# All mixture-of-experts blocks placed by matmul, 34 blocks a pass in place of 40, some split 96 and 32 rows

## The chip, the core and the metric

One core of one Trainium2 chip runs the whole step. The metric is device time in microseconds from one launch. Five engines work side by side: PE (TensorE; its weight loads are shown apart as PEld), DVE (VectorE), ACT (ScalarE), POOL (GpSimd) and SP (SyncE, which only issues DMAs here). Sixteen DMA engines serve the core.

## What is computed

The reference is one layer of a hybrid diffusion backbone over 128 context and 256 latent tokens of width 1024: attention and a recurrent branch, then a mixture of experts, then a final norm. The change is in the mixture of experts:

```python
t = h.reshape(B * T, D)                       # 384 tokens in all, D = 1024
# sigmoid routing, group-limited, TOP_K = 8 of N_EXPERTS = 64 -> gates (n, 64)
act = silu(einsum('nd,edf->nef', t, w_gate_e)) * einsum('nd,edf->nef', t, w_up_e) * gates[:, :, None]
routed = einsum('nef,efd->nd', act, w_down_e) # expert width 256
shared = (silu(t @ w_gate_s) * (t @ w_up_s)) @ w_down_s
x = x + gate_ffn * (routed + shared)
```

So 384 x 8 = 3072 token rows go to 64 experts of unequal load, and every expert's 3 MB of fp32 weights (w_gate, w_up, w_down, 1 MB each) come from HBM once.

## The kernel before

Stages. Up to about 335 us the kernel computes the adaLN vectors, the projections, attention, the recurrent branch and the merge. Around 340 us it routes: a count of each expert's rows, a sort of the experts by load, and tables from which every block of rows is picked. From 360 us on it works through blocks of 128 rows, in turns. The last 20 us are the final norm and the store.

Blocks. The experts are taken in four groups of 16. A block is of kind H (128 rows of one heavy expert) or L (64 rows each of two experts). A group is 4 H and 6 L, so 10 turns (`ORDER0` for the first group, `ORDER` for the others), and a pass is 40 turns. If an expert had more rows than its place holds, a further pass would run (`limits`, `more_i`); the runs here need one.

One turn, u, on PE, in program order: `gate_up(u)` (L1538: x_t against w_gate and w_up, 8 steps of the contraction, 512 columns moving; for H one matmul of 128 stationary columns a step, for L two of 64, on the two halves of the array, which write partitions 0-63 and 64-127 of one bank); `turn_tokens(u+1)` (L1526, 8 transposes of the next block's gathered rows); `down(u-1)` (L1557: 2 halves of 512 columns by 2 contraction steps, split by rows as above); two transposes of the activation (L1666); `block_rows(u+3)` (L1519, a small product that finds row numbers and gates of a later block); and, for a placed block, `place(u-1)` (L1576). An fp32 matmul stands in the trace as two records; an fp32r one, as in `place`, as one.

How a block's result returns to its tokens. There are two ways. A scattered block is scaled by its gates (ACT, y_sb) and added into y_dram by an indirect DMA that POOL issues (L792); each scatter waits until the one before has landed. y_dram is zeroed first (L713, 3 MB) and at the end read back in six DMAs of 512 KB (L599, L600) and summed by DVE. A placed block is split into a high and a low fp32r part (ACT L1094, DVE L2236) and multiplied by a 0/1 matrix made by DVE (L2224, token number against row): 3 token tiles x 2 halves x high and low = 12 matmuls of 128x512 (L1576); DVE then adds six banks into ffn_acc (L2247). 17 of the 40 blocks are placed: two of the first group (`FIRST_PLACED`), five of each later group (`PLACED`; in the last group `ENDING`, two of whose five are done in `place_ending`, L1601). 23 are scattered.

Order and buffers. Weights arrive in a ring of five slots of 3 MB (`ring`, `gu`, `dn`). SP issues an expert's w_gate and w_up when the slot's last user has finished `gate_up`, w_down when it has finished `down`. `gate_up(u+1)` writes a bank that the placement of the turn before used, so it waits for DVE's first sum; `turn_tokens` waits for all six. The shared expert's down product (`shared_down`, L1452) runs in turns 5, 6 and 7 of the first group, and the broadcast of gate_ffn (`spread`, L1189) in turn 4.

A place where the array is cut into 32-column tiles is L1178, in the adaLN stage: four matmuls of 32 stationary columns, 512 moving, on four quarters of the array.

Of the kernel before, what the change touches and what calls it, by code (L numbers as in the profile page):

```python
# [5 lines left out]
F32 = mybir.dt.float32  # L6
# [28 lines left out]
ORDER0, ORDER = "HHHHLLLLLL", "HLLHLHLLHL"  # L35
NGRP, EPG, BPG = 4, 16, 10
NPASS_BLK = NGRP * BPG
MAXPASS = 4
# [3 lines left out]
NBLK = NPASS_BLK * MAXPASS  # L42
NSIDE = 2 * NPASS_BLK
FIXED = 4
PLACED = (0, 2, 4, 5, 7)
SCATTERED = BPG - len(PLACED)
FIRST_PLACED = (BPG - 3, BPG - 2)
ENDING = (0, 2, BPG - 3, BPG - 2, BPG - 1)
HEAVY = 16
EMPTY = 1024  # L50
MARK = 4096.0
TABLES = 3 + 7
RC = 387
LAT0 = 131
NTAB = NBLK + 4
# [11 lines left out]
def hybrid_step(nc, x_prompt, x_sample, cache_k, cache_v, state_f, state_b, c, c_ctx,  # L67
# [5 lines left out]
    with ctx:  # L73
        KB = 1024
        arena = ctx.enter_context(nc.sbuf_tensor("arena", [P, 207 * 256 + 160], F32))
# [124 lines left out]
        shared_dn = at("shared_dn", [P, 2048], EX + 48)  # L200
# [4 lines left out]
        shared_sb = at("shared_sb", [P, D], EX + 56)  # L205
        x_t = at("x_t", [P, KD * CAP], EX + 108)
        zeros = at("zeros", [P, D], EX + 108)
        a_sh = at("a_sh", [P, TT, 2 * CAP], EX + 112)
        y_sb = [at(f"y_sb{i}", [P, D], EX + 116 + 4 * i) for i in range(2)]
# [31 lines left out]
        shift = little("shift", [P, 2, NSIDE])  # L241
        row_off = little("row_off", [P, 1])
        slot_row = little("slot_row", [P, UN], I32)
# [13 lines left out]
        seq_rank = little("seq_rank", [NE, NE])  # L257
        side_pick = little("side_pick", [NE, NSIDE])
        seq_pick = little("seq_pick", [NE, NE])
        inv_cap = little("inv_cap", [P, NSIDE])  # L260
        fill = little("fill", [P, NSIDE])
        place[0] = EX + 162.5
        limit[0] = EX + 163.5
        seq_expert = little("seq_expert", [1, MAXPASS * NE], I32)


        ffn = [at(f"ffn{t}", [P, D], EX + 4 * t) for t in range(TT)]
        ffn_b = [at(f"ffn_b{t}", [P, D], EX + 12 + 4 * t) for t in range(TT)]
# [3 lines left out]
        y_r = [at(f"y_r{i}", [P, D], EX + 116 + 4 * i, F32R) for i in range(2)]  # L272
        y_hi = [y_r[0], at("y_hi", [P, D], EX + 36, F32R)]
        y_lo_end = at("y_lo_end", [P, D], 12, F32R)
        y_lo = [at(f"y_lo{i}", [P, D], EX + 44 - 4 * i, F32R) for i in range(2)]
# [5 lines left out]

        y_dram = nc.dram_tensor("y_dram", (2 * NTOK, D), F32, kind="Internal").ap()

# [30 lines left out]
        for n, (kind, i) in enumerate(chunks):  # L314
# [3 lines left out]
        S = {n: sem(n) for n in """added cond_loaded vec_loaded cache_loaded bias_loaded block_loaded  # L318
# [10 lines left out]
            gates_made sides_mm sides_evac picks_made sorted_mm gu_used dn_used b_zero  # L329
            sh_mm sh_silu sh_act sh_at_mm sh_at shd_mm shd_evac shared_loaded early_mm  # L330
# [25 lines left out]
        def experts_of(order):  # L356

            n, blocks = 0, []
            for kind in order:
                blocks.append(tuple(range(n, n + 1 + (kind == "L"))))  # L360
                n += len(blocks[-1])
            assert n == EPG
            return blocks
# [3 lines left out]
        def shared_turn(u, first):  # L367

            return (u - FIRST_SHARED,) if first and FIRST_SHARED <= u < FIRST_SHARED + TT else ()

        def shared_outs(u):

            return bank[2 + (u + 1) % 2], bank[2 + u % 2]

        FIRST_SHARED = 5
        SHARED_BANK = (2, 3, 5)
        SPREAD_TURN = 4
# [5 lines left out]

        first_half = (("router_loaded", 16), ("shared_loaded", 48), ("bias_loaded", 32))

        def heavy_places(order):
            return [x[0] for x, kind in zip(experts_of(order), order) if kind == "H"]

        FIRST_FOUR = heavy_places(ORDER0)


        SLOT0 = [x % RING for x in range(EPG)]
        heavy_slot, light_slots = 3, (1, 2, 4, 0)
        SLOT, lights = [], 0
        for x in range(EPG):
            if x in heavy_places(ORDER):
                SLOT.append(heavy_slot)
            else:
                SLOT.append(light_slots[lights % 4])
                lights += 1  # L400
# [20 lines left out]
        assert not {SLOT[x] for x in turns[False][-1]} & {1, 2}  # L421
        assert [SLOT0[x] for x in turns[False][-1]] == [SLOT[x] for x in turns[False][-1]]

        assert max(PLACED) < UN - 2

        assert {SLOT[x] for x in turns[False][UN - 3]} == {1, 2}
        assert not {SLOT[x] for u in (UN - 2, UN - 1) for x in turns[False][u]} & {1, 2}

        def placed_in(last):
            return ENDING if last else PLACED  # L430

        def is_placed(u, first, last=False):
            return u in FIRST_PLACED if first else u % UN in placed_in(last and u >= 0)

        def first_scatters(u):

            return 16 * sum(v not in FIRST_PLACED for v in range(u))

        def scatters_ahead(b, u, last=False):

            back = 1 if u < 0 else 0
            here = placed_in(last and not back)
            return b * (16 * SCATTERED) + 16 * (len(PLACED) - len(FIRST_PLACED) - SCATTERED * back + sum(v not in here for v in range(u % UN)))

        def places_ahead(b, v, each, last=False, first=False):

            if first:
                return each * FIRST_PLACED.index(v)
            return b * (each * len(PLACED)) + each * (placed_in(last).index(v) + len(FIRST_PLACED) - len(PLACED))

        def low_rows(v, last):

            return y_lo_end if last and v == UN - 3 else y_r[1 - v % 2]
# [4 lines left out]

        def rows_of(x, order_x):

            return slice(0, P) if len(order_x) == 1 else slice(HALF * order_x.index(x), HALF * order_x.index(x) + HALF)
# [34 lines left out]
        def _(sp):  # L496
# [37 lines left out]
            def load_gu(x, group, e):  # L534
                k, y = slot_of(x, group is None), earlier(x, group is None)
                if group is None:
                    if y is not None:
                        sp.wait_ge(S["gu_used"], y + 1)
                    elif k == RING - 1:
                        sp.wait_ge(S["sh_mm"], TT)  # L540
                else:
                    sp.wait_ge(S["gu_used"], group * EPG + (y + 1))
                    sp.sem_inc(S["sp_turn"], 1)
# [4 lines left out]
            def load_dn(x, group, e):  # L548
                k, y = slot_of(x, group is None), earlier(x, group is None)
                if group is None:  # L550
                    if y is not None:
                        sp.wait_ge(S["dn_used"], y + 1)
                else:
                    sp.wait_ge(S["dn_used"], group * EPG + (y + 1))
                    sp.sem_inc(S["sp_turn"], 1)
# [6 lines left out]
            for g, w in enumerate((w_gate_s, w_up_s)):  # L562
                sp.dma_start(shared_gu[:, 2048 * g:2048 * g + 2048], w[0].rearrange("(p k) n -> p (k n)", k=KD)).then_inc(S["shared_loaded"], 16)
            sp.wait_ge(S["out_mm"], 12)
            for n, x in enumerate(FIRST_FOUR):
                if n == FIXED - 1:

                    sp.wait_ge(S["sides_mm"], 1)
                    sp.wait_ge(S["h2_stored"], 16 * TT)
# [5 lines left out]
            for u in range(BPG):  # L575
                now = [(x, expert_at(slice(x, x + 1))) for x in turns[True][u] if x not in FIRST_FOUR]
                for n, (x, e) in enumerate(now):
                    load_gu(x, None, e)
                    if x == FIXED:
                        sp.dma_start(shared_dn[:, :], w_down_s[0].rearrange("(p k) n -> p (k n)", k=2)).then_inc(S["shared_loaded"], 16)  # L580
# [4 lines left out]
            with sp.Fori(1, passes * NGRP) as b:  # L585
                late = [(x, expert_at(bass.ds(b * EPG + (x - EPG), 1))) for x in turns[False][-1]]
                for u in range(BPG):
                    now = [(x, expert_at(bass.ds(b * EPG + x, 1))) for x in turns[False][u]]
# [5 lines left out]
            sp.wait_ge(S["added"], scatters_ahead(passes * NGRP - 1, UN - 1, True))  # L594
            sp.sem_inc(S["sp_turn"], 1)
            sp.wait_ge(S["dn_used"], (passes * NGRP - 1) * EPG + (turns[False][UN - 3][-1] + 1))
            sp.sem_inc(S["sp_turn"], 1)
            for t in range(TT):
                sp.dma_start(ffn[t][:, :], y_dram[t * P:(t + 1) * P, :]).then_inc(S[first_half[t][0]], 16)  # L599
                sp.dma_start(ffn_b[t][:, :], y_dram[NTOK + t * P:NTOK + (t + 1) * P, :]).then_inc(rows_loaded[t], 16)  # L600
            for x in turns[False][-1]:
                load_dn(x, passes * NGRP - 1, expert_at(bass.ds(passes * NE + (x - EPG), 1)))
# [6 lines left out]
        def _(pool):  # L609
# [101 lines left out]
            pool.memset(zeros[:, :], 0.0).then_inc(S["zero_filled"], 1)  # L711
            pool.wait_ge(S["zero_filled"], 7)
            pool.dma_start(y_dram.rearrange("(t p) d -> p t d", p=P), zeros[:, :].unsqueeze(1).to_broadcast([P, 2 * TT, D])  # L713
                           ).then_inc(S["b_zero"], 16)
# [23 lines left out]
            late = NE - EPG  # L738
            side = lambda ap: ap[:, 2 * BPG:NSIDE].rearrange("p (g u h) -> p g u h", u=BPG // 2, h=2)
# [1545 lines left out]
```

## Time and profile before

| | |
|---|---|
| median of 3 runs | 927.61 us |
| lowest, highest | 926.42, 934.16 us |
| span of the profiled execution, first to last instruction | 925.6 us |
| median over the span | 2.0 us |
| PE busy | 876.7 us, 95% of the span |
| DMA moved | 294.24 MB, mean 318 GB/s |

In the rows, busy time is the union of an engine's instructions; matmuls overlap and their ends are modelled, so the distance between starts is the surer measure. In a line of the time order, `128*64 128x512 ... x32` is 32 records with 128 rows and 64 columns of the array in use and 512 moving columns, and the number in brackets is idle time before the line and what ended it.

### The profile page before, as it was taken

What the parts mean: (1) busy time and instruction counts of PE and PEld (TensorE: products, weight loads), DVE (VectorE), ACT (ScalarE), POOL (GpSimd) and SP (SyncE); (2) the same over time, 40 slices, a digit from 0 to 9 for tenths busy, and PEclk for the clock granted to TensorE, in tenths of its full rate; (3) what the DMA queues carried; (4) which work ended last, traced back from release to release, by engine and by line L of the source; (5) the groups of instructions that cost most, each with busy time, mean ns of one, the idle gap of its engine ahead of it and who ended that gap; (6) DMA issues with size and microseconds to landing.
All of it is one profiled execution on the core that took longest, in us unless ns stands there. A gap on an engine that the chain in (4) does not pass through costs nothing.

```text
span 925.6 us, 12174 instructions
## 1 busy us (share of the span) xinstructions
PE 876.7 (95%) x4185; PEld 513.0 (55%) x4185; DVE 436.2 (47%) x961; ACT 254.9 (28%) x417; POOL 138.6 (15%) x224
## 2 busy tenths in 40 slices
PE   4799999999999899999999999999999999999991
PEld 2387876899998765443344444444444444444440
DVE  1562493677666554233253442542344442433386
ACT  2536634444423431212211122122112112212211
POOL 7410000000002131122110111011111012012202
PEclk9799999999999999999999999999999999999996
DMA  9974885722237398899999999999999999999971
GB/s 353 350 266 172 302 292 211 159 92 65 79 131 267 138 417 310 271 348 406 379 404 420 404 401 402 421 391 406 409 408 409 421 394 408 411 407 400 404 319 68
DMA packets 82416, 294.24 MB, mean 318 GB/s; under 512 B 16876, under 2 KB 33320, under 8 KB 57408
## 3 DMA queue, kind: packets, MB, share of 16 engines
q1 hardware_dynamic: 62352, 263.21, 71.7%
q0 software_dynamic: 11312, 25.85, 9.4%
q10 hardware_dynamic: 8704, 4.54, 1.9%
q8 instruction: 30, 0.49, 0.2%
q14 instruction: 18, 0.15, 0.0%
HBM read 286.11 MB, written 20.71 MB: 332 GB/s over the span
## 4 chain that ended last, share of the span: by engine, by line
PE 75%; DMA 14%; DVE 4%; issue 3%; ACT 1%; SPq 0%; ACTq 0%; POOL 0%; DVEq 0%; POOLq 0%
PE bank L1538 26%; PE bank L1557 13%; PE bank L1150 8%; PE bank L1152 7%; PE bank L1151 7%; DMA y_dram<-y_sb,slot_row 5%; PE bank L1526 4%; DMA chunk_raw<-in_w_ada_dram 3%; DMA b_t<-in_b_ada_dram 2%; PE bank L1178 1%; DMA h_dram<-h_row 1%; DMA dn<-in_w_down_e_dram 1%; PE bank L1230 1%; PE bank L1452 1%; DMA xg<-h_dram,slot_tok 1%
## 5 line engine op out<-in xcount | busy, mean ns | idle before, releaser
L1538 PE MATMUL bank<-gu,x_t 128*64 128x512 f32 (+1 forms) x1024 | 283.8, 596 | 2.6 <-DVE ffn_acc L2247 1.8
L1538 PEld LDWEIGHTS bank<-gu,x_t 128*64 128x64 f32 (+1 forms) x1024 | 101.3, 150 | 160.7 <-issue 157.4
L1557 PE MATMUL bank<-dn,a_t 128*64 128x512 f32 (+1 forms) x512 | 145.4, 597 | 0.6 <-DMA dn<-in_w_down_e_dram 0.6
L2113 DVE TENSOR_TENSOR act_sb<-silu_sb,bank 128x256 f32<-128x256 f32 x40 | 16.8, 421 | 194.8 <-ACT silu_sb L1111 194.8
L1111 ACT ACTIVATE silu_sb<-bank 128x256 f32<-128x256 f32 x40 | 15.4, 385 | 316.1 <-PE bank L1538 316.1
L1557 PEld LDWEIGHTS bank<-dn,a_t 128*64 128x64 f32 (+1 forms) x512 | 48.5, 150 | 69.8 <-issue 68.8
L1150 PE MATMUL bank<-h_hi,chunk_lo 128*128 128x384 f32 x240 | 84.2, 351 | 0.0
L1152 PE MATMUL bank<-h_hi,chunk_hi 128*128 128x384 f32 x240 | 80.6, 336 | 0.0
L1151 PE MATMUL bank<-h_lo,chunk_hi 128*128 128x384 f32 x240 | 80.4, 335 | 0.0
L792 POOL DMA_INDIRECT y_dram<-y_sb,slot_row x23 | 38.5, 1674 | 259.7 <-DVE slot_row L1996 225.7
L780 POOL DMA_INDIRECT xg<-h_dram,slot_tok x40 | 41.5, 1037 | 197.5 <-DVE slot_row L1996 175.5
L475 DVE TENSOR_TENSOR chunk_lo<-chunk_raw,chunk_hi 128x2048 fp32r<-128x2048 f32 x25 | 57.1, 2287 | 15.8 <-ACT chunk_hi L469 15.7
L469 ACT ACTIVATE chunk_hi<-chunk_raw 128x2048 fp32r<-128x2048 f32 x25 | 47.7, 1914 | 42.5 <-PE bank L1152 42.3
L2129 DVE COPY a_t<-bank 128x256 f32<-128x256 f32 x40 | 16.9, 423 | 76.8 <-PE bank L1666 76.6
L1526 PEld LDWEIGHTS bank<-ident,xg 128*128 128x128 f32 x320 | 35.5, 140 | 27.3 <-issue 26.6
L1150 PEld LDWEIGHTS bank<-h_hi,chunk_lo 128*128 128x128 f32 x240 | 45.0, 188 | 7.1 <-issue 5.4
L2247 DVE TENSOR_TENSOR ffn_acc<-ffn_acc,bank 128x512 f32<-128x512 f32 x78 | 47.8, 683 | 0.4
L1576 PE MATMUL bank<-y_r,place_r 128*128 128x512 f32 x174 | 45.1, 401 | 1.2 <-DVE a_t L2129 1.1
L1094 ACT ACTIVATE y_sb<-bank,slot_gate 128x512 f32<-128x512 f32 x46 | 31.6, 687 | 51.9 <-PE bank L1557 50.6
L1151 PEld LDWEIGHTS bank<-h_lo,chunk_hi 128*128 128x128 f32 x240 | 45.1, 188 | 0.3
L1152 PEld LDWEIGHTS bank<-h_hi,chunk_hi 128*128 128x128 f32 x240 | 45.1, 188 | 0.0
L1526 PE MATMUL bank<-ident,xg 128*128 128x128 f32 x320 | 42.8, 277 | 0.6 <-DMA xg<-h_dram,slot_tok 0.6
(366 smaller groups left out, 1099.9 us busy)
## 6 DMA issues: line engine op xcount, KB each, us to landing
gu<-in_w_gate_e_dram SPq DMA_DIRECT2D x64, 1024.0 KB, 14.7
gu<-in_w_up_e_dram SPq DMA_DIRECT2D x64, 1024.0 KB, 18.1
dn<-in_w_down_e_dram SPq DMA_DIRECT2D x64, 1024.0 KB, 19.5
chunk_raw<-in_w_ada_dram SPq DMA_DIRECT2D x24, 1024.0 KB, 8.8
chunk_raw<-in_w_in_dram SPq DMA_DIRECT2D x18, 1024.0 KB, 5.4
chunk_raw<-in_w_out_dram SPq DMA_DIRECT2D x4, 1024.0 KB, 5.1
y_dram<-zeros POOLq DMA_DIRECT2D x1, 3072.0 KB, 18.6
chunk_raw<-in_w_pa_dram SPq DMA_DIRECT2D x2, 1024.0 KB, 5.1
```

The lines of the kernel that those rows point to most:

```text
L469: act.activation(chunk_hi[j % HIGHS][:, :], chunk_raw[slot[n]][:, :], ACT.Copy).then_inc(S["chunk_high"], 1)
L475: dve.tensor_tensor(chunk_lo[slot[n]][:, :], chunk_raw[slot[n]][:, :], chunk_hi[j % HIGHS][:, :].bitcast(F32), ALU.subtract).then_inc(S["c ...
L780: pool.indirect_dma_start(xg[u % 2][:, :], None, h2_dram[:, :], bass.IndirectOffsetOnAxis(ap=slot_tok[:, u % UN:u % UN + 1], axis=0), boun ...
L792: pool.indirect_dma_start(y_dram[:, :], bass.IndirectOffsetOnAxis(ap=slot_row[:, u % UN:u % UN + 1], axis=0), y_sb[u % 2][:, :], None, bou ...
L1150: pe.matmul(out, left[1], right[0], start=start, stop=False)
L1151: pe.matmul(out, left[0], right[1], start=False, stop=False)
L1152: return pe.matmul(out, left[0], right[0], start=False, stop=stop)
L1526: mm = pe.transpose(bank[k // 4][:, (k % 4) * P:(k % 4 + 1) * P], xg[u % 2][:, k * P:(k + 1) * P], ident[:, :])
L1538: mm = pe.matmul(bank[2 + u % 2][at_x, :].rearrange("p (g n) -> p g n", g=2), x_t[:, cols], wide[:, :, k, :], start=(k == 0), stop=(k == K ...
L1557: mm = pe.matmul(outs[half][at_x, :], a_t[:, cols], dn[slot_of(x, first)][:, wc], start=(k == 0), stop=(k == 1))
L1576: return pe.matmul(out[:, :], place_r[:, t * P:(t + 1) * P], y[:, halves[half]], start=start, stop=not start)
L2247: dve.tensor_tensor(ffn_acc[t][:, cols], ffn_acc[t][:, cols], out[:, :], ALU.add).then_inc(S["place_out"], 1)
```

## The change

All 34 blocks of a pass are placed; the scatters, y_sb, y_dram, its zeroing, its reading back and the sums over it are gone. There is a new kind, M: 96 rows of one expert and 32 rows of another. The first group is MMMHHLHLHL (10 turns), the others are MLLMLLML (8 turns each): 4 H, 12 M and 18 L. The 96 rows of an M run as a tile of 64 columns and one of 32, the 32 rows as a tile of 32 columns, so each step of `gate_up` and `down` is three matmuls, in the order 64, 32, 32.

The heavy experts by load take 128 rows (4), then 96 (9, and the three that are fixed for early loading), 64 (36) and 32 (12). The placement of every block waits on the same semaphores as placed blocks did, with y_hi and y_lo single buffers. `select` of an M is two DVE operations, not one. The shared down product stands before turn 0, in three banks in rotation, and ACT writes it straight into ffn_acc, so that the three multiplications and additions of `shared_add` on DVE are gone; `spread` moves to turn 0. The check whether a further pass is needed moves ahead of the second `select`. Weight slots are dealt in another order. POOL makes two more rank tables and clears xg. The ending scales ffn_acc and adds it to x_sb just before the last block (`sums_in`), and then only the last two blocks' product.

```diff
-ORDER0, ORDER = "HHHHLLLLLL", "HLLHLHLLHL"
-NGRP, EPG, BPG = 4, 16, 10
+WIDE, NARROW = 96, 32
+ORDER0, ORDER = "MMMHHLHLHL", "MLLMLLML"
+NGRP, EPG, BPG0, BPG = 4, 16, len(ORDER0), len(ORDER)
...
+        def tiles_of(x, u, first):
+
+            if kind_of(u, first) == "H":
+                return [slice(0, P)]
+            second = x != turns[first][u][0]
+            if kind_of(u, first) == "L":
+                return [slice(HALF * second, HALF * second + HALF)]
+            return [slice(WIDE, P)] if second else [slice(0, HALF), slice(HALF, WIDE)]
...
                 for k in range(KD):
                     for x in experts:
-                        at_x = rows_of(x, experts)
-                        cols = slice(k * CAP + at_x.start, k * CAP + at_x.stop)
                         wide = gu[slot_of(x, first)][:, :].rearrange("p (g k n) -> p g k n", g=2, n=FE)
-                        mm = pe.matmul(bank[2 + u % 2][at_x, :].rearrange("p (g n) -> p g n", g=2), x_t[:, cols], wide[:, :, k, :],
-                                       start=(k == 0), stop=(k == KD - 1))
+                        for at_x in tiles_of(x, u, first):
+                            cols = slice(k * CAP + at_x.start, k * CAP + at_x.stop)
+                            mm = pe.matmul(bank[2 + u % 2][at_x, :].rearrange("p (g n) -> p g n", g=2), x_t[:, cols], wide[:, :, k, :],
+                                           start=(k == 0), stop=(k == KD - 1))
...
                         for x in experts:
-                            at_x = rows_of(x, experts)
-                            cols = slice(k * CAP + at_x.start, k * CAP + at_x.stop)
                             wc = slice(k * D + 512 * half, k * D + 512 * half + 512)
-                            mm = pe.matmul(outs[half][at_x, :], a_t[:, cols], dn[slot_of(x, first)][:, wc], start=(k == 0), stop=(k == 1))
+                            for at_x in tiles_of(x, u, first):
+                                cols = slice(k * CAP + at_x.start, k * CAP + at_x.stop)
+                                mm = pe.matmul(outs[half][at_x, :], a_t[:, cols], dn[slot_of(x, first)][:, wc], start=(k == 0), stop=(k == 1))
...
-                    if u and is_placed(u - 1, first, last) and not (last and u == UN - 1):
-                        place(u - 1, b, last, first)
+                    if not (first and u == 0) and not (last and u == BPG - 1):
+                        place(i - 1, u)
...
+            pe.wait_ge(S["shared_dn_loaded"], 16)
+            shared_down(0)
+            shared_turn_act(2)
+            shared_down(1)
+            shared_down(2)
             block_turn(0, True)
...
-            pool.dma_start(y_dram.rearrange("(t p) d -> p t d", p=P), zeros[:, :].unsqueeze(1).to_broadcast([P, 2 * TT, D])
-                           ).then_inc(S["b_zero"], 16)
...
-            for t in range(TT):
-                sp.dma_start(ffn[t][:, :], y_dram[t * P:(t + 1) * P, :]).then_inc(S[first_half[t][0]], 16)
-                sp.dma_start(ffn_b[t][:, :], y_dram[NTOK + t * P:NTOK + (t + 1) * P, :]).then_inc(rows_loaded[t], 16)
```

## Rows read from the trace of the kernel before

**Rows 1.** The page: span, busy time by engine, and the clock and DMA lines of 40 slices.
```profile
span 925.6 us, 12174 instructions
...
PE 876.7 (95%) x4185; PEld 513.0 (55%) x4185; DVE 436.2 (47%) x961; ACT 254.9 (28%) x417; POOL 138.6 (15%) x224
...
PEclk9799999999999999999999999999999999999996
DMA  9974885722237398899999999999999999999971
```

**Rows 2.** The page, chain that ended last: by engine.
```profile
PE 75%; DMA 14%; DVE 4%; issue 3%; ACT 1%; SPq 0%; ACTq 0%; POOL 0%; DVEq 0%; POOLq 0%
```

**Rows 3.** PE in order of time, 640 to 675 us: start us, us, engine, line.
```profile
646.14 7.09 PE L1538 MATMUL bank<-gu,x_t 128*64 128x512 f32 x32
653.16 1.09 PE L1526 MATMUL bank<-ident,xg 128*128 128x128 f32 x8
654.09 3.60 PE L1557 MATMUL bank<-dn,a_t 128*128 128x512 f32 x8
657.52 0.39 PE L1666 MATMUL bank<-ident,act_sb 128*128 128x128 f32 x2
...
657.83 3.30 PE L1576 MATMUL bank<-y_r,place_r 128*128 128x512 f32 x12
661.29 7.09 PE L1538 MATMUL bank<-gu,x_t 128*64 128x512 f32 x32 [0.17 <-DVE ffn_acc L2247]
...
669.33 3.65 PE L1557 MATMUL bank<-dn,a_t 128*64 128x512 f32 x16
672.92 0.51 PE L1666 MATMUL bank<-ident,act_sb 128*128 128x128 f32 x2
...
673.34 1.96 PE L1538 MATMUL bank<-gu,x_t 128*128 128x512 f32 x4
```

**Rows 4.** PE in order of time, 318 to 420 us: turns of 128-row blocks.
```profile
381.26 7.11 PE L1538 MATMUL bank<-gu,x_t 128*128 128x512 f32 x16
...
392.83 7.11 PE L1538 MATMUL bank<-gu,x_t 128*128 128x512 f32 x16
```

**Rows 5.** Groups by line and form, 350 to 890 us: busy us, mean ns | idle.
```profile
L1576 PE MATMUL bank<-y_r,place_r 128*128 128x512 f32 x174 | 45.1, 401 | 1.2 <-DVE a_t L2129 1.1
...
L2247 DVE TENSOR_TENSOR ffn_acc<-ffn_acc,bank 128x512 f32<-128x512 f32 x78 | 47.8, 683 | 0.4
```

**Rows 6.** PEld, then PE, at 64.70 us: four tiles of 32 columns.
```profile
64.70 0.16 PEld L1178 LDWEIGHTS bank<-chunk_raw,cond_t 128*32 128x32 f32 x8 [0.25 <-issue]
...
64.70 1.92 PE L1178 MATMUL bank<-chunk_raw,cond_t 128*32 128x512 f32 x16
66.55 0.92 PE L1263 MATMUL bank<-xc,block_w 128*128 128x387 f32 x2
```

**Rows 7.** PE at 350.5 us: from 64x128 tiles to 64x1 and back.
```profile
349.72 0.89 PE L1464 MATMUL bank<-side_pick,gate_et 64*128 64x80 f32 x6
...
350.34 0.27 PE L1464 MATMUL bank<-side_pick,gate_et 64*128 64x80 f32 x1
350.54 0.21 PE L1503 MATMUL bank<-seq_pick,expert_no 64*1 64x64 f32 x1
...
350.74 0.33 PE L1504 MATMUL bank<-side_pick,load_et 64*128 64x80 f32 x1
```

**Rows 8.** Stretches of 25 us: busy us of each engine, clock, DMA share, GB/s.
```profile
475.00:500.00 25.00, 24.64 (x116) 11.97 (x115) 15.21 (x35) 4.33 (x7) 2.01 (x2) 1.00 1.02 424
...
625.00:650.00 25.00, 25.00 (x106) 10.82 (x104) 5.45 (x19) 4.71 (x8) 4.81 (x4) 1.00 1.02 408
```

**Rows 9.** Waits, 350 to 890 us, and the last turn in order of time.
```profile
DVE y_r L2236 <- DMA y_dram<-y_sb,slot_row: 21.2, 9, 3.6
...
899.55 3.65 PE L1557 MATMUL bank<-dn,a_t 128*64 128x512 f32 x16 [0.62 <-DMA dn<-in_w_down_e_dram]
...
912.25 1.23 DVE L2219 TENSOR_TENSOR ffn<-ffn,gate_ffn 128x1024 f32<-128x1024 f32 x1
```

More of the change, by code:

```diff
@@ L359, in experts_of @@
             for kind in order:
-                blocks.append(tuple(range(n, n + 1 + (kind == "L"))))
+                blocks.append(tuple(range(n, n + 1 + (kind != "H"))))
                 n += len(blocks[-1])
@@ L420, in hybrid_step @@
             assert earlier(x, False) >= 0 or earlier(x, False) + EPG >= max(y for y in range(EPG) if SLOT0[y] == SLOT[x])
[L421 to L453, printed above, removed]
+        assert [SLOT0[x] for x in turns[True][-1]] == [SLOT[x] for x in turns[False][-1]]
+        assert ORDER0[-1] == ORDER[-1] and AHEAD % 2 == 0 and UN % 2 == 0
         def place_outs(u):
             return [(0, 0, bank[2 + (u + 1) % 2]), (1, 0, bank[0]), (2, 0, bank[1]), (0, 1, bank[4]), (1, 1, bank[5]), (2, 1, bank[6])]
-        def rows_of(x, order_x):
-            return slice(0, P) if len(order_x) == 1 else slice(HALF * order_x.index(x), HALF * order_x.index(x) + HALF)
         def split_high(act, n):
@@ L574, in _ @@
             late = []
[L575 to L577 removed]
+            for u in range(BPG0):
+                now = [(x, expert_at(slice(2 * u + n, 2 * u + n + 1))) for n, x in enumerate(turns[True][u]) if x not in FIRST_LOADS]
+                for x, e in now:
                     load_gu(x, None, e)
[L579 to L580 removed]
                 for x, e in late:
@@ L797, in block_turn @@
             def block_turn(b, first, last=False):
-                for u in range(UN):
-                    i = u if first else b * UN + u
-                    if not last or u + 2 < UN:
+                for u in range(BPG0 if first else BPG):
+                    i = block_no(b, u, first)
+                    if not last or u + 2 < BPG:
                         pool.wait_ge(S["xgt_mm"], i + 1)
-                        gather(i + 2, u + 2)
-                    if first and u == FIRST_PLACED[0] + 1:
-                        pool.wait_ge(S["x2_ready"], TT)
+                        gather(i + 2, u + 2, col_of(u + 2, first))
+                    if first and u == 0:
+                        pool.wait_ge(S["shd_mm"], 2 * TT)
@@ L805, in block_turn @@
                         count(tok_no[:, :], [[1, NTOK]], 0).then_inc(S["zero_filled"], 1)
-                    if not (first and u == 0) and not (u and is_placed(u - 1, first, last)):
-                        scatter(i - 1, u - 1, first_scatters(u - 1) if first else scatters_ahead(b, u - 1, last))
-            gather(0, 0)
-            gather(1, 1)
+            gather(0, 0, col_of(0, True))
+            gather(1, 1, col_of(1, True))
             pool.wait_ge(S["passes_ready"], 1)
@@ L1125, in _ @@
             shared_silu(2)
+            for n in range(2 * TT):
+                shared_out(n)
             block_turn(0, True)
@@ L1561, in down, with product @@
                                 mm.then_inc(S["dn_half"], 1)
-            def place(v, b, last=False, first=False):
-                i, at_y = b * UN + v, v % 2
-                y_low = low_rows(v, last)
-                ahead = lambda each: places_ahead(b, v, each, last, first)
-                outs = place_outs(v + 1)
-                halves = [slice(0, 512), slice(512, 1024)]
+            halves = [slice(0, 512), slice(512, 1024)]
+            def product(out, at_t, y, half, start=False, stop=False, matrix=place_r):
+                return pe.matmul(out[:, :], matrix[:, at_t * P:(at_t + 1) * P], y[:, halves[half]], start=start, stop=stop)
@@ L1570, in place @@
+            def place(i, u):
+                outs = place_outs(u)
                 pe.wait_ge(S["x_first"], i + 3)
                 pe.wait_ge(S["x_second"], i + 3)
-                pe.wait_ge(S["place_made"], ahead(1) + 1)
-                def product(n, y, start):
-                    t, half, out = outs[n]
-                    return pe.matmul(out[:, :], place_r[:, t * P:(t + 1) * P], y[:, halves[half]], start=start, stop=not start)
-                pe.wait_ge(S["y_half"], ahead(1) + 1)
-                for n in range(3):
-                    product(n, y_r[at_y], True)
+                pe.wait_ge(S["place_made"], i + 1)
+                pe.wait_ge(S["y_half"], i + 1)
+                for t, half, out in outs[0:3]:
+                    product(out, t, y_hi, half, start=True)
@@ L2060, in _ @@
             shared_act(2)
-            rows = lambda pas: row_tab[:, pas * NPASS_BLK:(pas + 1) * NPASS_BLK, :, :]
-            kinds = lambda order, kind: [u for u, c in enumerate(order) if c == kind]
+            heavy = 2 * FIXED
+            halved = lambda ap, at: ap[:, at + 2:at + 2 + 12].rearrange("p (n k) -> p n k", k=4)
             def later_experts():
-                more = seq_expert[:, NE:MAXPASS * NE].rearrange("a (r x) -> a r x", x=NE)
+                more = seq_expert[:, NSIDE:NSEQ].rearrange("a (r x) -> a r x", x=NLATE)
```

667 lines of the change are left out of this document (293 added, 374 removed).

## The prediction

> **What bounds the kernel now.** I read the page first. PE is busy 95% of the span and its line of slices stands at 9 from the third on; from the 17th slice on the DMA engines are as full, and the clock is at its upper level throughout that part [rows 1]. The chain that ended last lies on PE for 75% [rows 2]. Two resources are full at once, so the order of time decides which one paces. In it the matmuls of the block stage follow each other with no idle time worth the name: between 646 and 673 us the reader sees one bracket, 0.17 us, and it names DVE's sum, not a weight load [rows 3]. So PE paces, and the transfers keep up with little to spare: a share of 1.02 at 408 to 424 GB/s [rows 8]. What the change is worth in the block stage is what it does to the sum of PE's turns.
>
> A turn is taken from start to start. Gate-up of a 64+64 block takes 653.16 - 646.14 = 7.02 us, down of a 128-row block 657.52 - 654.09 = 3.43, down of a 64+64 block 672.92 - 669.33 = 3.59, a placement 661.29 - 657.83 = 3.46. A whole turn without placement is 673.34 - 661.29 = 12.05 us between two L blocks [rows 3] and 392.83 - 381.26 = 11.57 between two H blocks [rows 4].
>
> **Part 1: six turns fewer, and fewer H.** Before, a pass is 16 H and 24 L: 16 x 11.57 + 24 x 12.05 = 474.3 us. After, were an M to cost what an L does, 4 x 11.57 + 30 x 12.05 = 407.8. That is -66.5 us, all of it on PE, so on the path [rows 3, 4].
>
> **Part 2: 17 more placements.** One costs 3.46 us in the row, and by the group 45.1 us / 174 records x 12 = 3.1 [rows 3, 5]. Between these ends (52.9 to 58.8 us for 17) I take 3.2, nearer to the group of many: +54.4. What comes with them on DVE, 6 sums of 0.683 us = 4.1 us a block [rows 5], lies beside the next gate-up of 7 us, and the row's 0.17 us is what is left of it [rows 3]. If that cover went, each turn would show more than this.
>
> **Part 3: the M blocks.** This is the term that decides. Per step of the contraction an L has two tiles of 64 columns, an M has one of 64 and two of 32. Equal tiles share a step's time. A 128-row down is 8 records in 3.43 us, 0.429 each; a 64+64 down is 16 records in 3.59, so two for the time of one plus 0.16 for the stretch; gate-up the same, 16 x 0.429 = 6.86 against 7.02 [rows 3]. Four tiles of 32 share it too: 16 records from 64.70 to 66.55, 1.85 us = 4 x 0.429 + 0.13 [rows 6]. The extra 0.13 to 0.16 us is paid once where the array passes from one size of tile to another and back. What no row shows is a tile of 64 and one of 32 together, on different columns.
>
> The nearest rows to it are a passage between two cut-up sizes: the last product of the 64x128 kind starts at 350.34, the first of the 64x1 kind at 350.54, the next of the 64x128 kind at 350.74 [rows 7]. The six of the first kind start from 349.72 to 350.34, 0.12 us apart, so of the 0.20 us to the next kind 0.08 go to the passage, of the size of the 0.13 to 0.16 that passing in and out costs above. I read that as: a change of size waits until the array is empty, whether the two sizes are both cut up or not. If that holds on disjoint columns too, the 64-column tile and the two of 32 cannot overlap: an M's step is 2 x 0.429 + 0.16 for the 64s, then 2 x 0.429 + 0.13 for the 32s, 2.01 us. Gate-up is 8 x 2.01 = 16.1 us against 7.02 (+9.1), down 4 x 2.01 = 8.0 against 3.59 (+4.4). 13.5 us x 12 M blocks = +162 us, no cover: gate-up and down are the path. The lower bound is 0 (all three share), the upper one three stretches in a row, +162 + 12 x 12 x (0.858 + 0.13) = +304. I take +162, since it follows the only rows with a change of size between cut-up tiles.
>
> The Trainium skill says it as a rule (page "TensorEngine Tiling (Array Packing)", sections "Available Configurations" and "Key Properties"): 128x64 and 128x32 are two configurations, and changing the mode, not merely the tile, drains the TensorE. The trace agrees as far as [rows 7] go. By the rule the time is the forecast, without it that of the first rival.
>
> **Part 4: what goes with the scatters.** DVE waited 21.2 us in all for a scatter to land, 9 times [rows 9], but PE was busy beside nearly all of it; I take -1 us (0 to -3). The 23 scatters, the 3 MB of zeros and six loads leave DMA and POOL; neither paces if M blocks are slow. With their share of the traffic gone, the three later groups need about 53.5 MB each (16 experts x 3 MB and a quarter of 3072 rows of 4 KB).
>
> **Part 5: the edges.** The shared down product and the broadcast move but keep their PE work: 0, with up to +3 if PE waits for the shared activation, for which the first shared_down gives 3.4 us of cover. The further-pass check is a few DVE operations of about 0.2 us ahead of the gather, which waits for the h2 store anyway: 0. At the end the 0.62 us wait for w_down and one of the multiplications of the last tile, 1.23 us, go [rows 9]: -1.8. `sums_in`, 6 DVE operations of 1.23, runs beside the last gate-up and down: 0, up to +3.
>
> **Sum.** -66.5 + 54.4 + 162 - 1 - 1.8 = +147.1. On the profiled execution's 925.6 us of span, and the 2.0 us by which the median lies above it, 1074.7 us. Its own range: 1037 if the passages between sizes cost nothing (12 x 12 x 0.858 = 124 in place of 162), 1088 with the dear placement, +4.4, the waits at both edges, +6, and 3 us of rounding of the step.
>
> **Rivals.**
> 1. *The mixed tiles share their step* (0.26). Nothing in the rows forbids it: the sharing tiles of [rows 3, 6] need disjoint columns, and 64, 32 and 32 are disjoint; the rate of records would be 24 in 3.43 us, less than the 16 in 1.85 of [rows 6]. Against it stand [rows 7]. Then -66.5 + 54.4 - 2.8 = -14.9: 912.7 us, faster. It decides as soon as an M's gate-up takes about 7 us, not 16. Within it the transfers may take over: a later group of 8 turns of about 15.25 us is 122 us, and 53.5 MB in it is 438 GB/s against the 424 of the best row [rows 8]; at 424 a group takes 126.1, +4.1 x 3 = +12 us: 925. The ring is full after the slow first group, which speaks for 913 to 920. A quarter of this case I put there.
> 2. *They overlap, but staggered*, three steps of 0.429 per contraction step where an L has two (0.06): 912.7 + 12 x 12 x 0.429 = 974.5. No row shows such a stagger; starts of equal tiles fall together [rows 6].
> 3. *Not even the two 32s pair* (0.02): 1074.7 + 142 = 1217. Against it, [rows 6].
> 4. *The change doesn't do in one pass what it says* (0.01): the places are smaller, and one row too many for an expert brings 32 more blocks, 20 x 15.25 + 12 x 28.75 = 650 us more. Routing the reference's inputs gives at most 124, 85, 78, 63 and 28 rows for places of 128, 96 (fixed), 96, 64 and 32, so it should not.
>
> **How the numbers follow.** Forecast 0.65; rivals 0.26, 0.06, 0.02, 0.01. To leave out no more than 2 in 10 the range must reach rival 1: 909 to 1088. Both signs hold chance; the forecast's own range is 1037 to 1088. Faster by over 1% (what a measurement of this kernel can tell from no change) is most of rival 1, 0.22; within 1% is its transfer-bound part, 0.04; the rest is slower, 0.74.
>
> **What would show it.** An M's gate-up, from its first start to the first transpose behind it, near 16 us and its down near 8, L blocks unchanged at 7.02 and 3.59; weight loads of the 64s and the 32s in separate bursts; the three later groups at about 162 us each; the DMA share falling from 1.02 to near 0.8 in them, as 53.5 MB in 162 us are 330 GB/s; PE without waits. An M's gate-up of 7 us proves the step of part 3 wrong, and then the DMA share stays at 1 and waits for gu or dn may show in the later groups. A placement far from 3.2 us would show part 2 wrong, turns beyond 34 part 1.

## The result, and the profile after

The changed kernel takes 1080.15 us (median of 4, 1074.39 to 1082.90) against 930.88 us (median of 4, 926.42 to 934.37) for the kernel before in the same measurement: 1.1598 times, 95% interval 1.1552 to 1.1645, slower. The profiled execution took 1074.39 us, of which 1072.6 are its span. Predicted were 1074.7 us, which is 1.1586 times the 927.61 that were shown.

The page of the changed kernel: span, busy time by engine, the clock and DMA lines of 40 slices, and the chain that ended last by engine.

```profile
span 1072.6 us, 12941 instructions
...
PE 1019.3 (95%) x4599; PEld 519.6 (48%) x4599; DVE 490.9 (46%) x1019; ACT 240.8 (22%) x393; POOL 94.3 (9%) x206
...
PEclk9899999999999999999999999999999999999997
DMA  9956766223529654747765988875988875988811
...
PE 86%; DMA 6%; DVE 4%; issue 2%; ACT 1%; POOL 0%; ACTq 0%; DVEq 0%; POOLq 0%
```

Beside [rows 1, 2] three things stand out. PE is still busy 95% of the span: its busy time grew by 1019.3 - 876.7 = 142.6 of the 147.0 us, so nearly all of the loss is time in which PE has an instruction open, not idle time. The chain lies on PE for 86% (75% before). And the DMA line, a row of 9s from the 17th slice on before, is now mostly 7s and 8s: the transfers wait for PE, not the other way.

PE of the changed kernel in order of time; the columns are those of [rows 3]. The first rows are turns 3 and 4 of the first group, the others turn 10, an M block, with a down of an L block behind it.

```profile
459.10 8.01 PE L1486 MATMUL bank<-dn,a_t 128*64 128x512 f32 x24
467.04 0.51 PE L1579 MATMUL bank<-ident,act_sb 128*128 128x128 f32 x2
...
467.46 1.19 PE L1495 MATMUL bank<-y_hi,place_r 128*128 128x512 f32 x4
...
470.10 0.39 PE L1495 MATMUL bank<-y_lo,place_r 128*128 128x512 f32 x1
472.57 8.80 PE L1467 MATMUL bank<-gu,x_t 128*128 128x512 f32 x16 [2.08 <-DVE ffn_acc L2107]
481.21 1.04 PE L1455 MATMUL bank<-ident,xg 128*128 128x128 f32 x8
...
568.56 15.95 PE L1467 MATMUL bank<-gu,x_t 128*64 128x512 f32 x48 [0.35 <-DVE ffn_acc L2107]
584.43 1.09 PE L1455 MATMUL bank<-ident,xg 128*128 128x128 f32 x8
585.46 3.65 PE L1486 MATMUL bank<-dn,a_t 128*64 128x512 f32 x16
589.04 0.50 PE L1579 MATMUL bank<-ident,act_sb 128*128 128x128 f32 x2
...
589.46 1.18 PE L1495 MATMUL bank<-y_hi,place_r 128*128 128x512 f32 x4
...
592.48 1.08 PE L1467 MATMUL bank<-gu,x_t 128*64 128x512 f32 x4
```

An M's gate-up takes 584.43 - 568.56 = 15.87 us (15.88 before rounding of the starts, as in most turns), its down 467.04 - 459.10 = 7.94; an L's down is still 589.04 - 585.46 = 3.58 and a placement 592.48 - 589.46 = 3.02. The forecast had 16.1, 8.0, 3.59 and 3.2.

PEld of the changed kernel in order of time, the start of that gate-up:

```profile
568.55 0.19 PEld L1467 LDWEIGHTS bank<-gu,x_t 128*64 128x64 f32 x2 [0.77 <-issue]
569.55 0.14 PEld L1467 LDWEIGHTS bank<-gu,x_t 128*32 128x32 f32 x4 [0.81 <-issue]
570.54 0.19 PEld L1467 LDWEIGHTS bank<-gu,x_t 128*64 128x64 f32 x2 [0.84 <-issue]
571.54 0.14 PEld L1467 LDWEIGHTS bank<-gu,x_t 128*32 128x32 f32 x4 [0.81 <-issue]
```

This is the view that decides between the theories. The load of the 64-column weights and that of the two 32-column weights never stand together: there is one burst each 0.98 to 1.00 us, and between them the weight loader is idle for 0.8 us. The profile shows nothing that its next load, which is for other columns, would wait for (`<-issue`). Two matmul records of 0.429 us [rows 3] run one after the other in each half step, and 0.13 us are left over.

Stretches of 25 us of the changed kernel (the columns are those of [rows 8]):

```profile
450.00:475.00 25.00, 21.73 (x69) 8.82 (x70) 13.07 (x33) 2.36 (x4) 0.99 (x1) 0.97 0.61 242
475.00:500.00 25.00, 22.76 (x89) 11.49 (x88) 11.15 (x30) 3.34 (x6) 0.99 (x1) 0.96 0.52 187
650.00:675.00 25.00, 24.58 (x107) 9.67 (x107) 12.05 (x25) 2.36 (x4) 1.98 (x2) 1.00 0.88 347
675.00:700.00 25.00, 24.84 (x99) 7.72 (x95) 7.93 (x17) 2.36 (x4) 0.99 (x1) 1.00 0.70 286
```

The last two show a DMA share of 0.88 and 0.70 where [rows 8] have 1.02. Over the first two later groups, 161.3 us each (568.56 to 729.87 and on to 891.26 us), the share is 0.81 at 329 GB/s; the forecast had about 162 us, 0.8 and 330. The first two lines show what it did not have: PE busy for only 21.7 and 22.8 of 25 us, and the granted clock under its upper level.

One thing is needed to compare executions. They differ by up to 8 us ahead of the block stage, in code that no kernel here changes: the first gate-up of the block stage starts between 368.9 and 377.0 us in the kernels with 34 blocks. So beside the medians I use the time from there to the end of the span. In the kernel before it takes in the shared down product, which the change moved ahead of that point.

| kernel | first gate-up | to the end of the span |
|---|---|---|
| before | 360.67 | 564.9, of which 10.8 are the shared down product |
| changed | 370.29 | 702.3 |
| two sizes, grouped | 376.27 | 676.5 |
| tables after the sums | 374.12 | 692.1 |
| three tiles of 32 | 376.98 | 550.2 |
| two tiles of 64 | 370.93 | 549.2 |
| tiles of 32 and tables after the sums | 368.91 | 540.3 |
| the same, half of w_up | 370.70 | 533.8 |

### The profile page after: what moved, and what is told of

It is laid out like the page before. It is cut to its first block, busy times and chain, and to the rows that moved or that the text cites. A ratio compares the mean times of both kernels' runs of the same rounds, so it can differ in the third digit from the quotient of the medians.

```text
span 1072.6 us, 12941 instructions
## 1 busy us (share of the span) xinstructions
PE 1019.3 (95%) x4599; PEld 519.6 (48%) x4599; DVE 490.9 (46%) x1019; ACT 240.8 (22%) x393; POOL 94.3 (9%) x206
## 3 DMA queue, kind: packets, MB, share of 16 engines
HBM read 279.82 MB, written 5.51 MB: 266 GB/s over the span
## 4 chain that ended last, share of the span: by engine, by line
PE 86%; DMA 6%; DVE 4%; issue 2%; ACT 1%; POOL 0%; ACTq 0%; DVEq 0%; POOLq 0%
PE bank L1467 33%; PE bank L1486 16%; PE bank L1078 6%; PE bank L1080 6%; PE bank L1079 6%; PE bank L1495 6%; PE bank L1455 3%; DMA chunk_raw<-in_w_ada_dram 3%; DMA b_t<-in_b_ada_dram 1%; PE bank L1106 1%; PE bank L1158 1%; PE bank L1579 1%; DMA h_dram<-h_row 1%; PE bank L1382 1%; PE bank L1191 1%
## 5 line engine op out<-in xcount | busy, mean ns | idle before, releaser
L1467 PE MATMUL bank<-gu,x_t 128*64 128x512 f32 (+2 forms) x1216 | 349.0, 603 | 13.5 <-DVE ffn_acc L2107 8.9
L1467 PEld LDWEIGHTS bank<-gu,x_t 128*64 128x64 f32 (+2 forms) x1216 | 88.2, 130 | 259.2 <-issue 256.3
L1486 PE MATMUL bank<-dn,a_t 128*64 128x512 f32 (+2 forms) x608 | 176.2, 603 | 0.0
L2107 DVE TENSOR_TENSOR ffn_acc<-ffn_acc,bank 128x512 f32<-128x512 f32 x192 | 117.7, 682 | 1.5 <-PE bank L1495 0.4
L1486 PEld LDWEIGHTS bank<-dn,a_t 128*64 128x64 f32 (+2 forms) x608 | 41.0, 130 | 111.3 <-issue 111.3
L2099 DVE SCALAR_TENSOR_TENSOR y_lo<-bank,slot_gate,y_hi 128x512 fp32r<-128x512 f32 x68 | 50.8, 747 | 79.6 <-ACT y_hi L1033 79.4
L1033 ACT ACTIVATE y_hi<-bank,slot_gate 128x512 fp32r<-128x512 f32 x68 | 46.8, 688 | 134.2 <-PE bank L1486 134.2
L1495 PE MATMUL bank<-y_hi,place_r 128*128 128x512 f32 x198 | 65.1, 409 | 0.0
L1495 PE MATMUL bank<-y_lo,place_r 128*128 128x512 f32 x198 | 61.4, 391 | 0.0
L1495 PEld LDWEIGHTS bank<-y_lo,place_r 128*128 128x128 f32 x198 | 37.1, 188 | 6.6
```

The costliest lines, as they stand in the source:

```text
L1033: act.activation(y_hi[:, half * 512:half * 512 + 512], bank[outs[half]][:, :], ACT.Copy, scale=slot_gate[:, col:col + 1]).then_inc(S["y_re ...
L1467: mm = pe.matmul(bank[2 + u % 2][at_x, :].rearrange("p (g n) -> p g n", g=2), x_t[:, cols], wide[:, :, k, :], start=(k == 0), stop=(k == K ...
L1486: mm = pe.matmul(outs[half][at_x, :], a_t[:, cols], dn[slot_of(x, first)][:, wc], start=(k == 0), stop=(k == 1))
L1495: return pe.matmul(out[:, :], matrix[:, at_t * P:(at_t + 1) * P], y[:, halves[half]], start=start, stop=stop)
L2099: dve.scalar_tensor_tensor(y_lo[:, cols], bank[outs[half]][:, :], slot_gate[:, col:col + 1], y_hi[:, cols].bitcast(F32), ALU.mult, ALU.sub ...
L2107: dve.tensor_tensor(ffn_acc[t][:, cols], ffn_acc[t][:, cols], out[:, :], ALU.add).then_inc(S["place_out"], 1)
```

## The experiments

The theory under test: a change of tile size waits until the array is empty, so the 64-column tile of an M never runs beside its two of 32, and that is nearly all of the loss. The rivals: the loss lies in M blocks whatever their tiles (a third matmul a step, more instructions, the placements), or in what else the change moves.

### All tiles of an M of one size

```
-            return [slice(WIDE, P)] if second else [slice(0, HALF), slice(HALF, WIDE)]
+            return [slice(WIDE, P)] if second else [slice(NARROW * n, NARROW * n + NARROW) for n in range(3)]
```

The 96 rows run as three tiles of 32 columns, so a step is four matmuls in place of three, all of one size. Everything else is the changed kernel.

> The only edit: the 96 rows run as three tiles of 32 columns, so an M block has four tiles of one size in place of 64, 32 and 32. Theory (a change of tile size waits until the array is empty, tiles of equal size share a step): an M's gate-up falls from 15.9 us to about 7.0 and its down from 7.9 to about 3.6, 12 x 13.2 = 158 us less, so about 920 us; if the transfers then become the bound (53.5 MB in a group of 122 us), up to 933, with waits for gu or dn and a DMA share of 1. Rival 1 (an M is slow since it has more tiles and records per step than an L, whatever their sizes): four tiles are no better than three, M gate-up at 16 us or above, 1080 us or more. Rival 2 (staggered sharing, a step of 0.429 us more for each tile past two): gate-up about 14 us, about 1050 us.

Measured: 927.0 us (median of 10, 921.49 to 929.03) against 934.02 (13 runs) for the kernel before, ratio 0.9923 (0.9893 to 0.9952). PE in order of time, an M's gate-up:

```profile
535.68 7.07 PE L1467 MATMUL bank<-gu,x_t 128*32 128x512 f32 x64 [0.35 <-DVE ffn_acc L2107]
542.68 1.09 PE L1455 MATMUL bank<-ident,xg 128*128 128x128 f32 x8
```

PEld in the same gate-up:

```profile
536.13 0.14 PEld L1467 LDWEIGHTS bank<-gu,x_t 128*32 128x32 f32 x4 [0.29 <-issue]
536.56 0.14 PEld L1467 LDWEIGHTS bank<-gu,x_t 128*32 128x32 f32 x4 [0.29 <-issue]
```

Stretches of 25 us:

```profile
650.00:675.00 25.00, 24.72 (x168) 10.87 (x168) 15.19 (x35) 4.33 (x7) 1.98 (x2) 1.00 1.01 420
```

64 records take 7.00 us where 48 took 15.88. More matmuls, less than half the time: the third matmul is not the cost, the second size is. Four weight loads now stand in one burst every 0.43 us. The M turns lost 8.88 us in gate-up and 4.37 in down (7.94 to 3.57), 159.0 us over 12, and the stretch to the end of the span 702.3 - 550.2 = 152.1; the difference is about what the transfers took back, for their share is at 1.01 again (below).

### The two sizes, but each only once a product

```
-                for k in range(KD):
+                for size, k in [(n, k) for n in (P, HALF, NARROW) for k in range(KD)]:
...
+                            if at_x.stop - at_x.start != size:
+                                continue
```

All steps of the 64-column tile come first, then all of the two 32s; in `down` likewise inside each half of the output. Tiles, products and traffic stay as in the changed kernel; what goes is the changes of size, 14 of the 16 of a gate-up and 4 of the 8 of a down.

> The same tiles, 64, 32 and 32, but in gate-up all 8 steps of the 64-column tile first and then all 8 steps of the two 32s (in down the same within each half of the columns), so the size changes once in a gate-up, not 15 times. Theory (no sharing across sizes, plus about 0.15 us for each passage): gate-up 16 x 0.429 + 0.16 + 16 x 0.429 + 0.13 = 14.0 us in place of 15.9, down 4 stretches of 4 x 0.429 + 0.15 = 7.5 in place of 7.9, 12 x 2.4 = 28 us less, about 1051 us. Rival (different sizes would share, and it is the many passages that cost): gate-up near 7 us, about 925 us.

Measured: 1051.2 us (median of 4, 1042.27 to 1054.62), ratio to before 1.1235 (1.1159 to 1.1312). PE in order of time:

```profile
570.35 14.06 PE L1469 MATMUL bank<-gu,x_t 128*64 128x512 f32 x48 [0.37 <-issue]
584.35 1.09 PE L1455 MATMUL bank<-ident,xg 128*128 128x128 f32 x8
```

PEld in the same gate-up, where the one size follows the other:

```profile
576.41 0.14 PEld L1469 LDWEIGHTS bank<-gu,x_t 128*64 128x64 f32 x1 [0.29 <-issue]
577.36 0.14 PEld L1469 LDWEIGHTS bank<-gu,x_t 128*32 128x32 f32 x4 [0.81 <-issue]
577.81 0.12 PEld L1469 LDWEIGHTS bank<-gu,x_t 128*32 128x32 f32 x2 [0.31 <-issue]
```

Gate-up is 14.00 us, down 7.40. This gives the price of a change of size: (15.88 - 14.00) / 14 = 0.134 us, and by the downs (7.94 - 7.40) / 4 = 0.135. With it the changed kernel's gate-up comes apart as 16 x 0.858 + 16 x 0.134 = 15.87: the changes are about 2.1 us of it, and the larger part of the loss, 130 us over 12 blocks by 14.00 - 7.00 and 7.40 - 3.57, is that the 64 does not run beside the 32s.

That larger part is shown by the changed kernel, where the sizes alternate in every step and a step still takes 1.985 us, and by the run with three tiles of 32. This run alone could not show it, and its rival (gate-up near 7 us) was badly put: here all 16 records of the 64 stand ahead of the 32s in the program, PE starts them in that order, and by the order alone no more than the last of them could run beside the first 32s. What it does show at that one place is that not even those do: within one size the loads come every 0.43 us, and across the change, from 576.41 to 577.36, it takes 0.95, with an idle gap of 0.81.

### Two tiles of 64

```
-            return [slice(WIDE, P)] if second else [slice(0, HALF), slice(HALF, WIDE)]
+            return [slice(HALF * second, HALF * second + HALF)]
```

An M is multiplied as an L is. This leaves out the product of rows 64 to 95 with the wide expert's weights; loads, placements and turns stay.

> An M block is multiplied as an L is, two tiles of 64 columns; this leaves out the product of rows 64 to 95 with the wide expert's weights (they meet the narrow expert's), everything else is unchanged. It measures what 34 placed blocks cost with no mixing at all. Theory: M turns as L turns, gate-up 7.0, down 3.6, about 920 us, the same as with four tiles of 32. Rival (something else in the 34-block plan costs too, such as the weight slots or the transfers): above 933 us.

Measured: 920.63 us (2 runs, 919.33 and 921.93), ratio 0.9868 (0.9802 to 0.9933). PE in order of time:

```profile
544.74 7.09 PE L1467 MATMUL bank<-gu,x_t 128*64 128x512 f32 x32
551.75 1.09 PE L1455 MATMUL bank<-ident,xg 128*128 128x128 f32 x8
```

7.01 us with 32 records, 7.00 with 64 of half the width. The stretch to the end is 549.2 us against 550.2 with three tiles of 32, so cutting the 96 rows fully costs nothing that can be seen. In the profiled executions the rest of the difference lies ahead of the block stage: first gate-up at 370.93 against 376.98.

### Tables after the sums

```
-                    if first:
-                        later_passes(u)
                     if placing and not ending:
                         place_sums(i - 1, u)
+                    if first:
+                        later_passes(u)
```

Only this is changed in the changed kernel. It is aimed at the 2.08 us in which PE waits ahead of turn 4. DVE of the changed kernel in order of time, before that gap:

```profile
469.09 0.55 DVE L1905 TENSOR_TENSOR onehot<-rank_of,rank_tab 128x384 bf16<-128x384 f32 x1
469.56 0.23 DVE L2003 COPY rank_tab<-rank_tab 128x144 f32<-128x144 f32 x1
469.82 0.17 DVE L2004 COPY rank_tab<-rank_tab 128x18 f32<-128x18 f32 x1
470.03 0.94 DVE L2008 TENSOR_SCALAR rank_tab<-rank_tab 128x3 f32<-128x3 f32 x4
471.01 0.58 DVE L2010 COPY rank_tab<-rank_tab 128x6 f32<-128x6 f32 x3
471.62 2.48 DVE L2107 TENSOR_TENSOR ffn_acc<-ffn_acc,bank 128x512 f32<-128x512 f32 x4
```

The nine small operations of `later_ranks` prepare a table for a further pass, which these runs do not need. They take from 469.56 to 471.62, 2.06 us, and stand in front of the first sum. `gate_up` of the next turn needs that sum's bank, and starts at 472.57.

> In the first group DVE adds the six sums of a placed block first and prepares the tables of further passes after them, in place of before. Theory (those 8 to 10 small operations keep the first sum, for which the next gate-up waits, and the pause of 2 us lowers the clock in turn 4): the placements of turns 2, 3 and 4 take about 3.3 us in place of 5.1 to 5.5, the gate-up of turn 4 takes 6.9 in place of 8.6, and turns 5 to 8 lose 0.5 each; 8 to 9 us less, about 1072 us. Rival (DVE has too much work in these turns in any order): the time stays at 1080 and the waits move to the next turn.

Measured: 1066.8 us (median of 4, 1065.00 to 1071.68), ratio to before 1.1441 (1.1374 to 1.1508), against 1.1598 of the changed kernel. DVE in order of time at the same turn:

```profile
470.56 0.55 DVE L1905 TENSOR_TENSOR onehot<-rank_of,rank_tab 128x384 bf16<-128x384 f32 x1
471.14 3.68 DVE L2107 TENSOR_TENSOR ffn_acc<-ffn_acc,bank 128x512 f32<-128x512 f32 x6
474.74 0.23 DVE L2003 COPY rank_tab<-rank_tab 128x144 f32<-128x144 f32 x1
```

The first sum follows the placement at once and the tables come behind the sums. PE in order of time there:

```profile
471.54 0.39 PE L1495 MATMUL bank<-y_lo,place_r 128*128 128x512 f32 x1
472.09 7.10 PE L1467 MATMUL bank<-gu,x_t 128*128 128x512 f32 x16 [0.16 <-issue]
479.03 1.04 PE L1455 MATMUL bank<-ident,xg 128*128 128x128 f32 x8
```

The stretch to the end is shorter by 702.3 - 692.1 = 10.2 us; 8 to 9 were expected. It comes out of two places. From the first product of a placement to the next gate-up, turns 2, 3 and 4 took 5.51, 5.11 and 5.23 us and now take 3.15, 3.16 and 3.27; turns 5 to 8 lost about 0.6 each, 8.6 us together. And the H gate-up of turn 4 is back from 481.21 - 472.57 = 8.64 us to 479.03 - 472.09 = 6.94: 1.7 us.

### Both edits together

The tiles of 32 and the tables after the sums.

> Both edits together: three tiles of 32 for the 96 rows, and the tables of further passes after the sums. Theory: the first group loses its waits, 9 to 14 us as in the run with that edit alone, but with equal tiles the three later groups run at the pace of the transfers (420 GB/s, share 1.01), and a first group that ends earlier has moved fewer weights ahead; so between 915 us (all of it kept) and 925 us (all of it taken back by the transfers), middle 919, ratio to before 0.98 to 0.99. Rival (the transfers set the end alone, whatever PE does): 927 us as without the second edit, more waits for gu in the last group.

Measured: 916.86 us (median of 6, 909.57 to 918.42) against 932.13 (11 runs) for the kernel before, ratio 0.9840 (0.9795 to 0.9884). It beats both kernels. All turns of the first group that place take about 15.1 us. What is left shows later. PE in order of time, two late gate-ups with the wait ahead of each:

```profile
826.29 7.09 PE L1467 MATMUL bank<-gu,x_t 128*64 128x512 f32 x32 [1.92 <-DMA gu<-in_w_up_e_dram]
...
842.17 7.09 PE L1467 MATMUL bank<-gu,x_t 128*64 128x512 f32 x32 [0.86 <-DMA gu<-in_w_up_e_dram]
```

The waits from 340 us on: the total in us, how many, and the longest.

```profile
PE bank L1467 <- DMA gu<-in_w_up_e_dram: 5.2, 6, 1.9
```

Stretches of 25 us:

```profile
800.00:825.00 25.00, 23.61 (x150) 11.25 (x146) 13.59 (x32) 4.72 (x8) 1.98 (x2) 1.00 1.02 420
825.00:850.00 25.00, 22.85 (x128) 10.41 (x129) 10.02 (x21) 2.75 (x5) 0.99 (x1) 1.00 1.01 419
```

The share is above 1 and PE waits for w_up: in the last third of the block stage the transfers pace, as the second half of rival 1 had it.

### The same, with half of w_up in the later groups

```
+                    n = 1024 if g and group is not None else 2048
```

Of each w_up of the three later groups only half is loaded, 25 MB less in all. This leaves out the values of that half; every instruction of PE stays.

> As the run before it, but the three later groups load only half of each w_up (this leaves out 48 x 0.5 MB = 25 MB of weights, so experts are multiplied with another's second half of w_up). It takes away a sixth of the later groups' traffic and no work of PE. Theory (equal tiles leave the later groups bound by transfers): no waits for gu, the DMA share in them falls to about 0.85, the groups fall to 122 us each, and the time to about 910 us. Rival (PE and DVE bound, the full DMA engines are no matter): the same time as the run before it, within 2 us.

Measured: 910.81 us (median of 5, 906.28 to 912.52), ratio 0.9793 (0.9745 to 0.9840). Stretches of 25 us:

```profile
800.00:825.00 25.00, 24.67 (x156) 11.48 (x156) 15.03 (x34) 4.64 (x8) 1.98 (x2) 1.00 0.96 379
825.00:850.00 25.00, 25.00 (x142) 10.50 (x138) 10.50 (x22) 4.16 (x8) 0.99 (x1) 1.00 0.90 352
```

No wait for a weight is left, and turns 24 to 31 take 15.0 to 15.3 us where they took 15.6 to 17.0. The share fell less than was expected: over the first two later groups, 121.7 us each, it is 0.92, not 0.85. The stretch to the end is 533.8 against 540.3: waiting for transfers costs the kernel with both edits 6.5 us.

## Why the prediction was right, point by point

**What bounds.** As said: PE paced before, and paces after; the DMA share fell with it, to 0.81. One sign failed: PE was to have no waits, and it waits 2.48, 2.08 and 2.24 us ahead of the gate-ups of turns 3, 4 and 5.

**Part 3, the M blocks.** Forecast 2.01 us a step, 13.5 us a block, +162. Measured 15.88 / 8 = 1.985 a step, and against an L 8.86 + 4.35 = 13.2 a block, +158.5. The small difference is the price of a change of size: the forecast took 0.16 and 0.13 from what passing in and out of a stretch costs, and it is 0.134 both ways (2 x 0.858 + 2 x 0.134 = 1.984). The reading of [rows 7], that a change between two cut-up sizes waits for the empty array, held on disjoint columns too, which no row had shown. The rule of the Trainium skill (page "TensorEngine Tiling (Array Packing)", section "Key Properties") that a change of mode drains the engine agrees with the 1.985 us a step. The same section has different tiles load and multiply in parallel; the trace agrees within one size (64 records in 7.00 us) and only there.

**Parts 1, 2, 4 and 5.** Forecast together -66.5 + 54.4 - 1 - 1.8 = -14.9. The last experiment has neither the M term, nor the tables, nor waits for transfers, so it shows these parts alone: 904.5 - 925.6 = -21.1 by the spans. Counted from the first gate-up it is 533.8 - (564.9 - 10.8) = -20.3; the other 0.8 lie ahead of the block stage. The largest piece of the 6 us between is the price of a placement. The forecast took 3.2 us for each of 17. From the first product of a placement to whatever PE does next, the 33 ahead of the last take 104.6 us in the kernel with its tables after the sums (3.17 each), but the 16 ahead of the last in the kernel before took 53.4 (3.34 each, one of them 4.38). The difference is 51.2, not 54.4. The other 3 us are spread over many turns and were not taken apart.

**The term that was missing.** Part 2 named DVE's 6 sums of a placement as hidden beside the next gate-up, with the words that each turn would show more if that cover went. Neither it nor Part 5, on the edges, asked what DVE does ahead of the sums in the first group. There both kernels build the tables for further passes (`later_passes`, turns 2 to 8). Before, turns 2 to 7 had no placement for them to delay; now every turn from 1 on has one. The tables stand in front of the sum that the next gate-up needs, and cost 10.2 us, 1.7 of them through the clock.

**The sum.** -21.1 + 158.5 + 10.2 = 147.6, and the profile shows 1072.6 - 925.6 = 147.0. The forecast was +147.1. That it is so close is partly luck: the M blocks cost 3.5 us less and the rest gained 6 us more than forecast, and the tables, not in the sum, took 10 back. Counted from the first gate-up, where the executions can be compared, the parts give -20.3 + 158.5 + 10.2 = 148.4, and the profiles show 702.3 - 554.1 = 148.2.

**The rivals.** Rival 1, tiles of two sizes sharing a step, is excluded by the bursts of PEld. Its arithmetic can still be tried, since four equal tiles share: 912.7 us where PE paces and 925 where transfers do, against 916.86 measured without the tables' delay. The transfer term was +12 and is 6.5. Rival 2, a stagger of three, needs 10.3 us for 8 steps, not 15.88. Rival 3 needs the two 32s apart; they start together. Rival 4 needs further blocks; 34 turns were run.

**Not tried.** One tile of 64 beside a single one of 32, which would show whether any two sizes can overlap on other columns; three tiles of one size, which would rule out that an odd number of tiles is what keeps them apart (the bursts and the 0.134 us at each change speak against it); another sharing out of the M blocks over the groups; and a pause of PE set by itself, to see from which length the clock falls.

## What to carry to other kernels

Cut the array into tiles of one size only within a stretch of matmuls: 96 + 32 rows as four tiles of 32 run in the time of two tiles of 64, as 64 + 32 + 32 they run in more than twice that (15.88 against 7.00 us), and sorting them by size gives back only 1.88 of the 8.88 us. A profile shows it at once as weight loads in separate bursts with a gap between them, while PE stands at 95% busy. And when work that was hidden in a turn meets a new wait in it, read the whole queue of the engine in front of the instruction that is waited for: here nine to eleven operations of about 0.2 us each held up PE by 2 us in each of three turns, and moving one call behind the sums gave it back.

## What the runs showed that was not expected

- The changed kernel's PE pauses for 2.48, 2.08 and 2.24 us ahead of the gate-ups of turns 3, 4 and 5, and after the second pause the granted clock was at its lower level for a time: 0.97 and 0.96 as means of two stretches of 25 us. At the lower level (1.2 GHz, half) that is 1.5 + 2 = 3.5 us at half speed, 1.75 lost, and the gate-up shows 1.70. In the kernel with its tables after the sums the longest of these pauses is 0.4 us and the clock 1.00. Which gate-up is hit differs: turn 4 in the changed kernel, turn 3 with three tiles of 32 (8.61 us), turns 3, 4 and 5 with the grouped order (8.41, 8.64, 8.55). So not every such pause is followed by the lower clock: in the changed kernel the gate-ups of turns 3 and 5 kept their 6.94 and 7.02 us. That the pauses bring it about is inferred from the two going together; they were not varied alone.
- The clock ahead of the block stage differs between executions of unchanged code: from 300 to 350 us it was 1.00 in the changed kernel's profile and 0.86 in that with three tiles of 32, whose first gate-up is 6.7 us later. A mean of 0.86 over 50 us is 14 us at the lower level, so 7 us lost, about that delay. The grouped order and the tables after the sums also have 0.86 there; the other profiles have 1.00.
- With both edits the transfers held 420 GB/s at a share of 1.01 as a mean from 540 to 870 us. Of the ceilings that the Trainium skill names (page "DMA: Bandwidth & Descriptors", section "Where 436 GB/s comes from"), 435 GB/s lies just above it and fits; the lower one of about 358 GB/s, the limit of HBM for one core, was passed here, where one core ran.
